# x loaded and weighted in four pieces around the first weight slot, with the S5 transposes one slot later

## The reference

```python
h = x + mixer(rmsnorm(x, norm_mix_g), w_in, ...)     # then cross attention, SwiGLU, and a second block of two layers

proj = xn @ w_in                                     # 1024 -> 2568 columns, the last 512 are u
# gated delta rule on q, k, v ...; beside it S5:
dt = exp(log_dt)
mag = exp(a_re * dt)
ab_re, ab_im = mag * cos(a_im * dt), mag * sin(a_im * dt)
co = ((ab_re - 1) + i ab_im) / (a_re + i a_im)       # "s5_coef" in the kernel
bb = co * b                                          # complex, per state and channel
x_t = ab * x_(t-1) + bb @ u_t ;  y_t = Re(c x_t) + d * u_t
```

## Time and profile before

| | us |
|---|---|
| median of 3 runs | 1184.15 |
| the three runs | 1183.84, 1184.15, 1184.19 |
| the profiled execution | 1185.06 |
| its span in the profile | 1183.3 |

### The profile page before, as it was taken

How to read it: one execution, slowest core, us unless ns; L and a number is a source line. 1 busy time by engine, 2 the same in 40 slices (tenths; PEclk the granted TensorE clock), 3 DMA queues, 4 the chain that set the end, 5 groups by cost and what they waited for, 6 DMA issues and landing times.

```text
span 1183.3 us, 21936 instructions
## 1 busy us (share of the span) xinstructions
PE 1161.7 (98%) x8694; PEld 1046.6 (88%) x8694; DVE 851.1 (72%) x1519; ACT 660.2 (56%) x1144; POOL 217.2 (18%) x135
## 2 busy tenths in 40 slices
PE   9999999999999999999999999999899999999997
PEld 8888889999888888798898899999799888999996
DVE  6997956745766766677787776767755577777776
ACT  4346556645544544565667555555755566555555
POOL 2030000201032322010011223231111201323230
PEclk9999999999999999999999999999999999999998
DMA  8433334535656565543344555565433443565651
GB/s 349 134 117 107 126 118 160 166 94 179 203 184 199 179 194 184 159 125 110 123 143 137 167 185 190 184 191 178 161 125 124 130 158 107 182 194 179 196 178 53
DMA packets 53253, 188.47 MB, mean 159 GB/s; under 512 B 5792, under 2 KB 7968, under 8 KB 52640
## 3 DMA queue, kind: packets, MB, share of 16 engines
q1 hardware_dynamic: 53152, 187.07, 49.1%
HBM read 186.00 MB, written 1.05 MB: 158 GB/s over the span
## 4 chain that ended last, share of the span: by engine, by line
PE 88%; DVE 6%; ACT 4%; issue 1%; DMA 0%; POOL 0%; ACTq 0%; DVEq 0%
PE banks L491 58%; PE banks L521 7%; PE banks L982 7%; PE banks L984 4%; DVE w_lo L1918 1%; PE banks L1059 1%; PE banks L1073 1%; ACT w_hi L1290 1%; PE banks L1039 1%; ACT arena L1752 1%; PE banks L612 1%; PE banks L1176 1%; PE banks L916 1%; PE banks L893 1%; DVE a_parts L1930 1%
## 5 line engine op out<-in xcount | busy, mean ns | idle before, releaser
L491 PE MATMUL banks<-a_parts,w_hi 128*128 128x256 f32 x2288 | 421.0, 285 | 3.3 <-DVE a_parts L1930 1.5
L1290 ACT ACTIVATE w_hi<-w_raw 128x1024 fp32r<-128x1024 f32 x313 | 329.0, 1052 | 157.6 <-PE banks L491 100.5
L491 PEld LDWEIGHTS banks<-a_parts,w_hi 128*128 128x128 f32 x2288 | 358.6, 191 | 12.2 <-issue 4.4
L2831 POOL TENSOR_TENSOR w_lo<-w_raw,w_hi 128x1024 fp32r<-128x1024 f32 x77 | 186.9, 2427 | 753.5 <-ACT w_hi L1290 753.5
L491 PE MATMUL banks<-a_parts,w_lo 128*128 128x256 f32 x1144 | 323.4, 283 | 0.0
L1918 DVE TENSOR_TENSOR w_lo<-w_raw,w_hi 128x1024 fp32r<-128x1024 f32 x236 | 290.8, 1234 | 38.3 <-ACT w_hi L1290 37.1
L491 PEld LDWEIGHTS banks<-a_parts,w_lo 128*128 128x128 f32 x1144 | 219.1, 192 | 0.0
L491 PE MATMUL banks<-w_hi,b_parts 128*128 128x512 f32 x416 | 130.7, 395 | 3.5 <-DVE b_parts L2558 3.1
L982 PE MATMUL banks<-b_parts,w_hi 128*128 128x512 f32 x352 | 125.2, 398 | 0.0
L1752 ACT ACTIVATE arena<-arena,pars 128x256 f32<-128x256 f32 x88 | 52.9, 601 | 120.7 <-DVE arena L2523 120.7
L491 PE MATMUL banks<-b_parts,w_hi 128*128 128x256 f32 x576 | 106.9, 287 | 0.8 <-DVE b_parts L2382 0.7
(11 more groups left out here) (423 smaller groups left out, 1528.0 us busy)
## 6 DMA issues: line engine op xcount, KB each, us to landing
w_raw<-in_weights SPq DMA_DIRECT2D x342, 512.0 KB, 3.4
arena<-in_mem SPq DMA_DIRECT2D x2, 1024.0 KB, 9.8
h<-in_x SPq DMA_DIRECT2D x1, 1024.0 KB, 6.1
early<-in_mem SPq DMA_DIRECT2D x1, 1024.0 KB, 14.9
out_h<-h SPq DMA_DIRECT2D x8, 128.0 KB, 2.0
cons<-in_cons SPq DMA_DIRECT2D x1, 546.0 KB, 8.6
arena<-in_late SPq DMA_DIRECT2D x1, 448.0 KB, 4.0
pars<-in_pars SPq DMA_DIRECT2D x1, 290.5 KB, 2.8
```

The costliest lines, as they stand in the source:

```text
L491: ins = mm(out, l, r, start=start and n == 0, stop=stop and n == 2, skip_group_check=check)
L1290: do(WHI[:, ring(n), :], RAW[:, n % RAW_SLOTS, :], ACT.Copy).then_inc(*inc("w_hi_made", ("w_hi", n)))
L2831: g.tensor_tensor(WLO[:, ring(n), :], RAW[:, n % RAW_SLOTS, :], WHI[:, ring(n), :].bitcast(F32), ALU.subtract).then_inc(*inc("w_lo_pool", ...
```

## The change

- SP loads x in four pieces of two feature tiles (256 KB each): the first ahead of slot 0, the other three ahead of slot 1. Each piece has its own semaphore (`x_part`).
- VectorE weighs the two tiles of a piece as soon as its small steps have come to a given place (`x_gained`): the first pair ahead of the wait for exp(log_dt), the second behind the fourth small step, the third behind the four L1952 steps, the last in the middle of the eight L1955 steps.
- ScalarE squares the tiles of a piece when that piece is there, and loads its table set for the logarithm ahead of the wait for cons.
- PE has 12 warm-up products for 19. `s5_turn` stands behind slot 4, `s5_lag0` behind slot 5.

```diff
--- before.py
+++ after.py
@@ -29,7 +29,7 @@
 RAW_SLOTS = 6
 SPLIT_SLOTS = 3
 NEG = -1e9
-WARM_UP = 19
+WARM_UP = 12
 TWO_PI = 2 * np.pi
 SIN_2PI = 6.283185
 ROUND = 12582912.0
@@ -437,8 +437,18 @@
         @block.sync
         def _(sp):
             sp.dma_start(PARS[:], io["pars"]).then_inc(*inc("pars_landed", "pars", by=16))
-            sp.dma_start(H[:], io["x"]).then_inc(*inc("x_landed", "x", by=16))
+
+
+            def x_part(c):
+
+                m = slice(2 * c, 2 * c + 2)
+                sp.dma_start(H[:, m, :], io["x"][:, m, :]).then_inc(*inc(f"x_landed{c}", ("x_in", c), by=16))
+
+            x_part(0)
             for s in range(SLOTS):
+                if s == 1:
+                    for c in range(1, 4):
+                        x_part(c)
                 if s == 2:
                     sp.dma_start(CONS[:], io["cons"]).then_inc(*inc("cons_landed", "cons", by=16))
                 if s == 3:
@@ -849,10 +859,10 @@
                     fm(name, j, x, lambda k: ("whole", ready, k), ahead_of={4: middle} if middle else ())
                 else:
                     tok_slot(name, j, x, lambda k: ("whole", ready, k), middle=middle)
-                if s == 3:
+                if s == 4:
                     pe.wait_ge(*at("cons"))
                     s5_turn()
-                if s == 4:
+                if s == 5:
                     s5_lag0()
                 if s - 1 in L2_AT:
                     delta_l2(L2_AT[s - 1])
@@ -1346,9 +1356,9 @@
             silu_set()
             s5_trig()
             for m in range(KD):
-                square("x", m, H[:, m, :], "x")
+                square("x", m, H[:, m, :], ("x_in", m // 2))
+            ln_exp()
             act.wait_ge(*at("cons"))
-            ln_exp()
             rstd("x", R)
             silu_set()
             act.wait_ge(*at("c_re"))
@@ -1943,20 +1953,29 @@
             v.tensor_tensor(den, a_re, a_re, ALU.mult)
             v.tensor_tensor(SMALL[:, 208:224], a_im, a_im, ALU.mult)
             er, fr = SMALL[:, 16:32], SMALL[:, 64:80]
+
+            def x_gained(c):
+
+                dve.wait_ge(*at(("x_in", c)))
+                for m in (2 * c, 2 * c + 1):
+                    v.tensor_scalar(XG[:, m, :], H[:, m, :], par("g_mix", m), None, ALU.mult).then_inc(
+                        *inc("gained", ("whole", "x", m)))
+
+            x_gained(0)
             dve.wait_ge(*at("s5_dt"))
             step(v.tensor_tensor(er, a_re, SMALL[:, 0:16], ALU.mult))
             step(v.tensor_scalar(er, er, -88.0, 88.0, ALU.max, ALU.min))
             step(v.tensor_scalar(er, er, 1.0 / 256, None, ALU.mult))
             step(v.tensor_scalar(fr, er, 1.0 / 720, None, ALU.mult))
+            x_gained(1)
             for coef in (1.0 / 120, 1.0 / 24, 1.0 / 6, 0.5):
                 step(v.scalar_tensor_tensor(fr, fr, coef, er, ALU.add, ALU.mult))
+            x_gained(2)
             step(v.scalar_tensor_tensor(er, fr, 1.0, er, ALU.add, ALU.mult))
             for n in range(8):
+                if n == 4:
+                    x_gained(3)
                 step(v.scalar_tensor_tensor(er, er, 2.0, er, ALU.add, ALU.mult), *(["s5_expm1"] if n == 7 else []))
-            dve.wait_ge(*at("x"))
-            for m in range(KD):
-                v.tensor_scalar(XG[:, m, :], H[:, m, :], par("g_mix", m), None, ALU.mult).then_inc(
-                    *inc("gained", ("whole", "x", m)))
             step(v.tensor_tensor(den, den, SMALL[:, 208:224], ALU.add))
             v.reciprocal(den, den).then_inc(*inc("vector_step", "s5_den"))
             v.tensor_tensor(par("g_both", n=8), par("g_fin", n=8), par("g2_mix0", n=8), ALU.mult)
```

## The result

| | before | changed |
|---|---|---|
| median of 11 runs each, us | 1184.15 | 1189.16 |
| lowest and highest | 1183.38, 1186.38 | 1187.38, 1193.94 |
| the profiled execution | 1185.06 | 1189.27 |
| its span | 1183.3 | 1187.5 |

The ratio of the means is 1.0042, 95% interval 1.0031 to 1.0054: slower by 5 us. The forecast was 1186.3 with a range up to 1187.8: too low, and its likeliest class, within 0.2% of no change, was wrong.

A forecast was written before the change was run, and what follows sets the result against it. PE, busy 98% of the span, was taken as the bound, so only its waits count: +1.69 before slot 3 and +0.37 at slot 4 make +2.1 us on the median 1184.15, giving 1186.3, range 1184.6 to 1187.8.

The forecast's parts named there:

- its likeliest class: Whole kernel: time within 0.2% (2.4 us) of no change, chance 0.54.
- The chain: VectorE to GpSimd to PE: eighth small step 3.79 us later, s5_coef at 17.53, s5_inputs +1.69, slot 3 at 21.87.
- GpSimd's chain late: GpSimd's small steps up to s5_coef: start 3.79 us later, at 11.30, take 6.23 instead of 6.48, end at 17.53.
- slot 3 behind the accumulator: PE before slot 3: waits for VectorE to empty slot 1's accumulator, starting at 21.87 instead of 20.18, +1.69 us.
- no give-back behind that: PE after 33.67 us: runs almost without a gap in unchanged order, so the difference carries to the end.
- the sum: PE up to the first S5 input products: 1.69 before slot 3 plus 0.37 at slot 4, +2.1 us.
- The later transposes: PE at slot 4, now ahead of the transposes: must have slot 2's accumulator, at 24.37 instead of 24.00, +0.37 us.
- the early start: PE's first product 2.1 us earlier, wholly given back as waits: about 1.3 in slot 0, 1.6 before sum_x, 1.9 before slot 3.
- part 1: Loads: x's second piece lands at 6.7 us, between 6.07 and 7.29; slot 0 at 6.1 to 6.7, last piece at 8.0.
- the late piece as a rival: Loads: second piece lands as late as 7.29, +2.7 us in all, 1186.9, slower by over 0.2%; chance 0.34.
- Part 2: PE's start: with seven fewer warm-up products, slot 0's weights set the first product at about 6.5, 2.1 us earlier.
- The clock: PE at slot 3: idling 1.9 us before it drops the clock to 1.2 GHz, +3.7 us more, 1190.0; chance 0.07.

The follow-up runs named there:

- the experiment: Changed kernel with s5_turn back behind slot 3 and s5_lag0 behind slot 4; measured once: 1189.12 us, beside 1187.15 of the kernel before.
- eight pieces: Kernel before with x in eight loads of 128 KB, one ahead of slot 0, seven behind; timed once: 1185.85 us, beside 1187.15 of the kernel before.
- rows of their own: Changed kernel with each piece of x one block in memory: median 1188.47 against 1185.59 of the kernel before, ratio 1.0027; also in a later version, 1184.07.
- the halves: Kernel before with x in two loads of 512 KB around slot 0; timed once: 1186.05 us, beside 1187.15 of the kernel before.

## Why the prediction was wrong

**What held.** The chain, step by step: weighings ahead of the eighth step, GpSimd's chain late, its length (6.23 forecast, 6.14 measured), VectorE waiting for it ahead of L2000, slot 3 behind the accumulator, no give-back behind that. With the measured start of the second pair in place of the assumed one, the sum is 2.06 + 2.13 = 4.19 up to the first S5 input products; 4.06 was measured. For slot 3 alone the sum gives 1.69 + 2.13 = 3.82, as measured, but this exactness is luck: `s5_inputs` began 0.20 earlier than that sum has it (19.48 for 19.68), and took 0.20 longer. The later transposes cost 0.24 (0.37 forecast), as the experiment confirms (0.23). That the early start would be given back held, and it was smaller still.

**The step that failed** is in part 1: "Its landing is therefore at the latest about 7.29". It took for granted that the same bytes in the same order take the same time, however x is cut. Six profiles with the same cut have the second piece at 8.0 to 8.9, 8.78 in the changed kernel, where the sum had 6.7 and at most 7.29. I had supported the bound by b_re and b_im, which land 0.59 us apart (13.06 and 13.65); but they land behind a full queue, where the loads move at 396 to 427 GB/s (the kernel before, 6 to 14 us). From 3 to 6 us the same kind of load didn't: 229 GB/s in the changed kernel. The 1.2 us by which x stood behind the rate of its followers was, by its semaphore steps, the tail of the load (eighth step at 5.9, last at 7.3), and slot 0's load behind it has the like (7.2, 8.6). The range was closed by that bound: the late piece as a rival ended at +2.7, and its place, price and slope were right, its end wrong by 1.5 us. The Trainium skill (DMA: Bandwidth & Descriptors, section Bandwidth) advises loads of 1 MiB and more for three quarters of the peak. The traces agree on the direction of the rate (364 to 396 GB/s from 3 to 6 us with x in one load, 208 to 296 with it cut), while eight pieces coming in sooner than four is not what a rule on size alone would give.

**Part 2** (first product at 6.5) fell with it: slot 0's weights landed at 8.06, not 6.1 to 6.7. That cost nothing, since the wait in front of slot 3 covers it; the kernel with rows of their own, which did start at 6.49, shows that.

**The clock** was in the forecast as a rival before slot 3, and there it didn't fall: in the changed kernel it is 1.00 through that wait. It did fall in other kernels' profiles, behind the idle stretch ahead of the first product.

**What is left.** The profiles account for 4.2 us, the medians are 5.0 apart, and lowest against lowest is 4.0. The changed kernel's 11 runs scatter over 6.6 us, those of before over 3.0. Some of the last 0.8 us is probably the clock. Nine of the fourteen profiles of this case, but neither of these two, have a stretch of low clock between 128 and 148 us (last section); from the first S5 input products to the end of the span they take 1150.5 us in the mean, the five others 1149.3. If it falls in more of the changed kernel's runs than of the other's, the medians move apart by a part of that. The mean clocks fit in part (1193.94 at 0.994, 1187.38 at 0.998, but 1190.16 at 0.998 too). Only one run of each kernel has a profile, so this is not shown. It also stays open why the first loads are slow when x is cut.

## What to carry to other kernels

A step that is put ahead of another on the same engine delays everything that waits for the other: look for the longest chain that starts behind the place of insertion, here sixteen small steps on another engine, and count its slack first. Don't bound a landing at the start of a program by rates measured behind a full queue, nor take one profile's landing for a fixed number: x in one load landed at 6.3, 6.8 and 7.3. An early piece that is wanted on an engine which has other work makes that work wait too. And where a wait is for an accumulator, ask first whether it can be emptied in the middle of the work that stands ahead of it.

## What the runs showed of the hardware

- Cutting one 1 MB load into pieces lowered the rate in the first microseconds: from 3 to 6 us the mean was 364 to 396 GB/s in the three profiles with x whole, 208 to 296 in the nine with pieces cut out of 8 KB rows, 297 and 336 in the two with rows of their own (4 KB rows in the halves, 1 KB in the eight pieces, 2 KB in the others). With x whole the landing still differed by a microsecond between profiles, 7.3, 6.3 and 6.8, while the eighth of its 16 semaphore steps came at 5.9 to 6.0 in all three.
- The clock can be low while PE is busy all the time. In the profile of the kernel with the weighings behind the steps:

```profile
130.00:134.00 4.00, 4.00 (x64) 3.35 (x66) 3.59 (x11) 2.26 (x3) 0.00 (x0) 0.63 0.40 141
134.00:138.00 4.00, 4.00 (x41) 2.98 (x34) 2.91 (x11) 1.90 (x5) 0.00 (x0) 0.94 0.07 28
```

PE is busy 4.00 of 4.00 us, here and in the two windows of 4 us ahead of it, and the granted clock is 0.63; the work there is many short products. Nine of the fourteen profiles have such a stretch once between 128 and 148 us, five do not: in the changed kernel's the windows from 125 to 160 read 1.00.
- Beside VectorE's sums of two tensors a GpSimd step of 128x16 took 0.77 (L2823 above) where the same form takes 0.22 later on; before, the one that began with these sums took 0.71. The sums moved by 3.5 us and held whichever steps stood beside them. It goes both ways: GpSimd's cast behind the chain took 0.81 beside the products of S5, 0.29 before, and two of these products (L2001, L2002) took 0.78 and 0.77, the others 0.68 or 0.69.
